# HGRN scans with the decays multiplied out ahead, the copy behind the query product, and 64 moving columns

## The reference

```python
def step(S, inp):
    qc, kc, vc, lc = inp
    bcum = jnp.cumsum(lc, axis=1)
    diff = bcum[:, :, None] - bcum[:, None, :]
    decay = jnp.where(lower, jnp.exp(jnp.where(lower, diff, 0.0)), 0.0)
    att = jnp.einsum('bthd,btshd->bths', qc, decay * kc[:, None])
    o = jnp.einsum('bths,bshv->bthv', att, vc) + jnp.einsum('bthd,bhdv->bthv', qc * jnp.exp(bcum), S)
    blast = bcum[:, -1]
    S_new = jnp.exp(blast)[..., None] * S + jnp.einsum('bshd,bshv->bhdv', kc * jnp.exp(blast[:, None] - bcum), vc)
    return S_new, o
```

## Time and profile before

| what | value |
|---|---|
| median of 3 runs | 2461.57 us |
| profiled execution, its own time | 2460.36 us |
| its span, first to last instruction | 2458.2 us |
| mean granted TensorE clock | 0.979 of full speed |
| TensorE matmul busy | 2296.2 us (93%) |
| VectorE busy | 1481.1 us (60%) |
| ScalarE busy | 832.3 us (34%) |
| POOL busy | 176.4 us (7%) |
| level matmuls (L789) | 1120 records, 291 ns of one |
| masked copies of the levels (L1819) | 140, 520 ns of one |
| decay products (L1823) | 120 on `tp` with 377 ns of one, 20 on `fg` |
| query products (L1825) | 120 on `tp` with 412 ns of one, 20 on `fg` |
| POOL's key products (L2149) | 120 on `tp` with 656 ns of one, 20 on `fg` with 854 |

### The profile page before, as it was taken

The page is one execution under the profiler, slowest core; times in us unless marked ns, Lnnn a source line. Parts: engine busy times, 40 slices in busy tenths (PEclk is TensorE's granted clock), DMA queues, the critical chain, the costliest instruction groups (busy, mean ns, idle before and its releaser), DMA issues.

```text
span 2458.2 us, 35437 instructions
## 1 busy us (share of the span) xinstructions
PE 2296.2 (93%) x14713; PEld 2019.9 (82%) x14713; DVE 1481.1 (60%) x2254; ACT 832.3 (34%) x1581; POOL 176.4 (7%) x217
## 2 busy tenths in 40 slices
PE   5989889988999889999999999999899999999998
PEld 3868868878888788779999999799555799999997
DVE  4457482257423777677555564789677575555655
ACT  4355372210122006444222222533455442222222
POOL 0000000023101330110000000200000100000002
PEclk9989999999999999999999999999999999999999
DMA  7411205510252002232222132131000022221321
GB/s 294 165 35 57 78 1 210 204 62 1 75 208 103 10 17 84 82 103 80 67 86 78 60 95 69 39 98 61 22 1 2 26 78 69 86 78 54 101 68 44
DMA packets 43854, 193.60 MB, mean 79 GB/s; under 512 B 5008, under 2 KB 5008, under 8 KB 36912
## 3 DMA queue, kind: packets, MB, share of 16 engines
q1 hardware_dynamic: 41472, 178.10, 21.5%
q0 software_dynamic: 2224, 13.24, 1.5%
HBM read 183.72 MB, written 7.60 MB: 78 GB/s over the span
## 4 chain that ended last, share of the span: by engine, by line
PE 81%; DVE 13%; ACT 3%; issue 2%; DMA 1%; SPq 0%; DVEq 0%; ACTq 0%
PE pg L843 30%; PE pg L882 17%; PE pg L638 16%; PE ps L789 3%; PE ps L1062 2%; PE pg L1042 2%; DVE att L1819 2%; PE ps L612 2%; DVE wk L1825 1%; PE ps L734 1%; PE pg L1017 1%; DMA ybuf<-in_wada 1%; DVE tp L1823 1%; PE ps L1017 1%; PE ps L753 1%
## 5 line engine op out<-in xcount | busy, mean ns | idle before, releaser
L843 PE MATMUL pg<-hh,xhi 128*128 128x320 f32 (+2 forms) x1008 | 314.4, 312 | 6.5 <-DVE hl L1635 6.5
L843 PE MATMUL pg<-hl,xhi 128*128 128x320 f32 (+2 forms) x1008 | 310.9, 308 | 0.0
L843 PE MATMUL pg<-hh,xlo 128*128 128x320 f32 (+2 forms) x1008 | 310.9, 308 | 0.0
L1521 DVE TENSOR_TENSOR wlo<-ring,whi 128x1024 fp32r<-128x1024 f32 x129 | 157.0, 1222 | 187.9 <-ACT whi L1105 187.7
L638 PE MATMUL pg<-hh,whi 128*128 128x320 f32 x976 | 238.8, 326 | 22.5 <-DVE hl L1553 9.5
L638 PE MATMUL pg<-hl,whi 128*128 128x320 f32 x976 | 225.5, 313 | 0.0
L638 PE MATMUL pg<-hh,wlo 128*128 128x320 f32 x976 | 225.1, 312 | 0.0
L638 PEld LDWEIGHTS pg<-hh,whi 128*128 128x128 f32 x976 | 165.2, 192 | 61.9 <-issue 51.4
L843 PE MATMUL pg<-hh,whi 128*128 128x320 f32 (+2 forms) x672 | 209.3, 311 | 3.3 <-DVE hl L1635 3.3
L843 PE MATMUL pg<-hl,whi 128*128 128x320 f32 (+2 forms) x672 | 207.2, 308 | 0.0
L843 PE MATMUL pg<-hh,wlo 128*128 128x320 f32 (+2 forms) x672 | 207.2, 308 | 0.0
(11 more groups left out here) (317 smaller groups left out, 4629.1 us busy)
## 6 DMA issues: line engine op xcount, KB each, us to landing
ring<-in_wstream SPq DMA_DIRECT2D x231, 512.0 KB, 3.7
adaring<-in_wada SPq DMA_DIRECT2D x21, 1024.0 KB, 5.0
ybuf<-in_wada SPq DMA_DIRECT2D x21, 1024.0 KB, 4.9
adabig<-in_wada SPq DMA_DIRECT2D x6, 1024.0 KB, 18.8
xk<-in_x SPq DMA_DIRECT2D x1, 2560.0 KB, 11.2
yssd_scratch<-ybuf POOLq DMA_DIRECT2D x2, 1280.0 KB, 5.8
xk<-yssd_scratch POOLq DMA_DIRECT2D x1, 2560.0 KB, 10.1
xk<-in_x_tok POOLq DMA_DIRECT2D x1, 2560.0 KB, 8.9
```

The source lines that it names most:

```text
L843: last = nc.tensor.matmul(out, w[:, k * P:(k + 1) * P], h[:, k, a:b], start=k == 0 and m == 0, stop=k == KT - 1 and m == 2)
L1521: V.tensor_tensor(lo, flat(ring[:, s % RING]), hi.bitcast(F32), ALU.subtract).then_inc(wlo_ready, 1)
```

## The change

Five things change in the scan.

The products of the gates of whole runs are no longer computed inside the levels. A new function `decays(p)` computes those of a whole pair of blocks: two products for level 1, one for each direction, and then one instruction for both directions at each further level. It runs before the first pair's `start`, and for every other pair at the end of the levels of the pair before. So that the old and the new products can stand side by side, they alternate between `tp` and a part of `sq` (`tps`).

The query product of a level stands ahead of the masked copy instead of behind it. It waits for the same `lv_ready`.

The matmul of a level takes as its moving side only the queries of the later runs, 64 columns a head instead of 128. Its output is packed: 64 columns a head.

The outputs of the levels alternate between two PSUM banks for each direction (`level_bank`), 0 and 2 of `ps` for direction 0, 1 and 3 for direction 1. Banks 2 and 3 also hold an output and a state sum, so TensorE waits at level 1 until the previous pair's are read. The diagonals move to bank 0 of `ps` for direction 0 and to the first bank of `pg` for direction 1.

A new semaphore, `lv_copied`, counts the masked copies. TensorE waits on it ahead of the diagonals and of the outputs; the copy of a level waits for that of the level before.

The diff:

```diff
@@ -308,6 +308,7 @@
             att = sb("att", [P, 2, HG_SET, P], F32, ph)
             hst = sb("hst", [P, 2, HG_SET, P], F32, ph)
             hfin = sb("hfin", [P, 2, HG_SET, P], F32, ph)
+        tps = [tp, flat(sq[:])[:, 0:2 * HG_SET * P].rearrange("p (d h t) -> p d h t", d=2, h=HG_SET)]
         qp = wk[:, 0:2, 0:HG_SET * P].rearrange("p d (h t) -> p d h t", h=HG_SET)
         ktok = wk[:, 2:4, 0:HG_SET * P].rearrange("p d (h t) -> p d h t", h=HG_SET)
         mask_in = ybuf[:, 0:2].rearrange("p f t -> p (f t)")[:, 0:2 * LEVELS * 64 + P]
@@ -476,6 +477,7 @@
         qp_ready = sem("qp_ready")
         dg_ready = sem("dg_ready")
         lv_ready = sem("lv_ready")
+        lv_copied = sem("lv_copied")
         kk_ready = sem("kk_ready")
         kt_ready = sem("kt_ready")
         kt_done = sem("kt_done")
@@ -542,10 +544,22 @@
 
             return ap.rearrange("p h (b t w) -> p h b t w", t=2, w=w)[:, :, :, t, :]
 
-        def tlevel(d, i):
+        def tlevels(np_, i):
 
             off = P - (P >> (i - 1))
-            return tp[:, d, :, off:off + (P >> i)]
+            return tps[np_ % 2][:, :, :, off:off + (P >> i)]
+
+        def tlevel(np_, d, i):
+
+            return tlevels(np_, i)[:, d]
+
+        def level_bank(d, i):
+
+            return ps[:, d + 2 * (i % 2), 0:HG_SET * 64]
+
+        def diagonal_bank(d):
+
+            return pg[:, 0, 0:512] if d else ps[:, 0, :]
 
         def mod_at(layer, part, ft, c):
             i = (layer * 6 + part) * KT + ft
@@ -768,8 +782,9 @@
                     for d in range(2):
                         if np_:
                             pe.wait_ge(qp_ready, qp_need(np_ - 1, 0, 0))
+                            pe.wait_ge(lv_copied, 2 * LEVELS * np_ - 1)
                         for h in range(HG_SET):
-                            last = nc.tensor.matmul(pg[:, 0, d * 512 + h * P:d * 512 + (h + 1) * P], kg[:, d, h, tok[d]],
+                            last = nc.tensor.matmul(diagonal_bank(d)[:, h * P:(h + 1) * P], kg[:, d, h, tok[d]],
                                                     qs[:, h, tok[d]], start=True, stop=True)
                         last.then_inc(dg_ready, 1)
 
@@ -780,14 +795,19 @@
                     if np_:
                         pe.wait_ge(o_done[1], np_)
                     for i in range(LEVELS):
+                        w = 1 << i
+                        if i == 1 and np_:
+                            pe.wait_ge(o_done[0], np_)
+                            pe.wait_ge(hs_done, 2 * (np_ - g) - 1 if p else 8)
                         for d in range(2):
                             n = (np_ * LEVELS + i) * 2 + d
                             pe.wait_ge(qp_ready, qp_need(np_, i, d))
                             if i:
                                 pe.wait_ge(kk_ready, n - 1)
                             for h in range(HG_SET):
-                                last = nc.tensor.matmul(ps[:, d, h * P:(h + 1) * P], kg[:, d, h, tok[d]],
-                                                        qp[:, d, h, :], start=True, stop=True)
+                                last = nc.tensor.matmul(level_bank(d, i)[:, h * 64:(h + 1) * 64]
+                                                        .rearrange("p (b w) -> p b w", w=w), kg[:, d, h, tok[d]],
+                                                        halves(qp[:, d], w, 1 - d)[:, h], start=True, stop=True)
                             last.then_inc(lv_ready, 1)
                     for d in range(2):
                         v = 2 * (np_ - g) + d
@@ -805,6 +825,7 @@
                     if p < len(HG_PAIRS) - 1:
                         diagonals(p + 1)
                     for d in range(2):
+                        pe.wait_ge(lv_copied, 2 * LEVELS * np_ + 2 * (LEVELS - 1) + d + 1)
                         if np_:
                             pe.wait_ge(o_done[d], np_)
                         if p == 1:
@@ -1792,6 +1813,19 @@
                 V.tensor_tensor(ybuf[:, 4 * g:4 * g + 4], ybuf[:, 4 * g:4 * g + 4], zs[:], ALU.mult).then_inc(yz_ready, 1)
 
             def hgrn(g):
+                def decays(p):
+
+                    np_ = g * len(HG_PAIRS) + p
+                    for d in range(2):
+                        tok = slice(HG_PAIRS[p][d] * P, (HG_PAIRS[p][d] + 1) * P)
+                        pairs = fg[:, d, :, tok].rearrange("p h (b t) -> p h b t", t=2)
+                        last = V.tensor_tensor(tlevel(np_, d, 1), pairs[:, :, :, 0], pairs[:, :, :, 1], ALU.mult)
+                    for i in range(1, LEVELS):
+                        link(last)
+                        pairs = tlevels(np_, i).rearrange("p d h (b t) -> p d h b t", t=2)
+                        last = V.tensor_tensor(tlevels(np_, i + 1), pairs[:, :, :, :, 0], pairs[:, :, :, :, 1], ALU.mult)
+                    link(last)
+
                 def start(p):
 
                     np_ = g * len(HG_PAIRS) + p
@@ -1802,9 +1836,10 @@
                         V.tensor_tensor(qp[:, d], qs[:, :, tok], fg[:, d, :, tok], ALU.mult).then_inc(qp_ready, 1)
                         dve.wait_ge(dg_ready, 2 * np_ + d + 1)
                         V.copy_predicated(att[:, d], m8[:, 2 * LEVELS * 64:].unsqueeze(1).broadcast_to([P, HG_SET, P]),
-                                          pg[:, 0, d * 512:(d + 1) * 512]
-                                          .rearrange("p (h t) -> p h t", h=HG_SET)).then_inc(qp_ready, 1)
-
+                                          diagonal_bank(d).rearrange("p (h t) -> p h t", h=HG_SET)
+                                          ).then_inc(qp_ready, 1)
+
+                decays(0)
                 start(0)
                 for p, pair in enumerate(HG_PAIRS):
                     np_ = g * len(HG_PAIRS) + p
@@ -1816,14 +1851,18 @@
                             dve.wait_ge(lv_ready, n + 1)
                             mo = (d * LEVELS + i) * 64
                             mask = m8[:, mo:mo + 64].rearrange("p (b w) -> p b w", w=w).unsqueeze(1)
+                            decay = fg[:, d, :, tok[d]] if i == 0 else tlevel(np_, d, i)
+                            decay = decay.rearrange("p h (b t) -> p h b t", t=2)[:, :, :, d]
+                            q = halves(qp[:, d], w, 1 - d)
+                            V.tensor_tensor(q, q, decay.unsqueeze(3).broadcast_to([P, HG_SET, 64 // w, w]),
+                                            ALU.mult).then_inc(qp_ready, 1)
+                            if i:
+                                dve.wait_ge(lv_copied, n - 1)
                             V.copy_predicated(halves(att[:, d], w, 1 - d), mask.broadcast_to([P, HG_SET, 64 // w, w]),
-                                              halves(ps[:, d].rearrange("p (h t) -> p h t", h=HG_SET), w, 1 - d))
-                            tot = fg[:, d, :, tok[d]] if i == 0 else tlevel(d, i)
-                            pairs = tot.rearrange("p h (b t) -> p h b t", t=2)
-                            V.tensor_tensor(tlevel(d, i + 1), pairs[:, :, :, 0], pairs[:, :, :, 1], ALU.mult)
-                            q = halves(qp[:, d], w, 1 - d)
-                            V.tensor_tensor(q, q, pairs[:, :, :, d].unsqueeze(3)
-                                            .broadcast_to([P, HG_SET, 64 // w, w]), ALU.mult).then_inc(qp_ready, 1)
+                                              level_bank(d, i).rearrange("p (h b w) -> p h b w", h=HG_SET, w=w)
+                                              ).then_inc(lv_copied, 1)
+                    if p < len(HG_PAIRS) - 1:
+                        decays(p + 1)
                     for d in range(2):
                         v = 2 * np_ + d
                         if d == 1 and p < len(HG_PAIRS) - 1:
@@ -1849,7 +1888,7 @@
                             dve.wait_ge(hst_in, 16 * (g + 1))
                             for h in range(HG_SET):
                                 last = V.scalar_tensor_tensor(out=hst[:, d, h], in0=hst[:, d, h],
-                                                              scalar=tlevel(d, LEVELS)[:, h], in1=src[:, h],
+                                                              scalar=tlevel(np_, d, LEVELS)[:, h], in1=src[:, h],
                                                               op0=ALU.mult, op1=ALU.add)
                             last.then_inc(hs_done, 1)
 
@@ -2143,7 +2182,7 @@
                             n = (np_ * LEVELS + i) * 2 + d
                             tok = slice(pair[d] * P, (pair[d] + 1) * P)
                             pool.wait_ge(lv_ready, n + 1)
-                            tot = fg[:, d, :, tok] if i == 0 else tlevel(d, i)
+                            tot = fg[:, d, :, tok] if i == 0 else tlevel(np_, d, i)
                             tot = tot.rearrange("p h (b t) -> p h b t", t=2)[:, :, :, 1 - d]
                             k = halves(kg[:, d, :, tok], w, d)
                             G.tensor_tensor(k, k, tot.unsqueeze(3).broadcast_to([P, HG_SET, 64 // w, w]),
```

## The result

The changed kernel takes 2521.73 us, the median of 4 runs (2519.38 to 2526.02), beside 2462.12 us before (4 runs). The ratio is 1.0244, 95% interval 1.0226 to 1.0262: 59.6 us slower, where 2436 us and a gain of 26 was forecast. The outcome is rival C, a lower TensorE clock.

The account below looks back on a forecast made before the run. In the scans TensorE and VectorE were both taken as nearly full, alternating in each level's chain, with POOL beside them. Savings of 20 and 5.6 us summed to 25.6, giving a median of 2436 us, range 2418 to 2456.

Parts of the forecast that it names:

- rival C: TensorE's clock in the scans falls to 1.2 GHz; 40 levels at that clock give 30 us slower, 2492; chance 0.09.
- Item 2: Level matmuls with 64 moving columns: the weight load sets the step, so only 0.05 us saved per direction, bounds 0 to 0.45.
- Item 1: Levels 1 to 6: query product before copy, decays out, POOL held 0.25 us; 12.94 instead of 14.04, 1.10 us a pair.
- Item 3: Level 0 of the third pair: query product first saves 1.23 and 1.44 us by direction; with levels 2.54 a pair.
- Item 4: Second pair of each half: query product ready before POOL's DMAs, less TensorE idle; 2.8 us a pair, bounds 1.9 to 3.6.
- Item 5: Decays ahead, 2.5 us a block, hide in VectorE's idle time between pairs and before the first pair: cost 0.
- Item 6: New waits, copies before diagonals and outputs and level 1 into banks 2 and 3: cost 0.
- A: No collisions in the levels: POOL is not set back, each of 60 levels gains 0.25 more, 15 us, 2421; chance 0.15.
- B: Levels keep 2.34 us because POOL and VectorE collide more than once; only level 0 gains, 13, 2449; chance 0.16.
- D: Decays don't hide at the start of a pair: 25 us back, 2461, no change; chance 0.05.
- forecast: The main case for the whole kernel: 25.6 us saved, 2436 us, own spread 2430 to 2443; chance 0.55.

Follow-up runs that it names:

- mixed run: Changed kernel with 128 moving columns at levels 0, 2, 4 and 6 and 64 at levels 1, 3 and 5: 2448.41 us, ratio 0.9943.
- run 16: Not a run's label: in "the mixed run 16 records take 1.97 us" the 16 counts matmul records; the run meant is the mixed run.
- 128-column kernel: Changed kernel with the level matmuls back at 128 moving columns a head, outputs unpacked, two banks and new order kept: 2442.45 us, ratio 0.9923.
- decays in PSUM: With 64 columns: the kernel with early first-pair decays and the query product's decays copied to PSUM, given the changed kernel's matmul: 2500.91 us, ratio 1.0159.
- PSUM run: Kernel with 128 columns and each half's first decays early, plus the decays the query product reads copied into a free PSUM bank: 2431.09 us, ratio 0.9865.
- key first: Kernel with 128 columns, masked copy ahead of the query product again, so POOL's key product starts first: 2446.49 us, ratio 0.9936.

## Why the prediction was wrong, point by point

**Item 2 is the step that failed.** It valued 64 columns at -0.05 us a direction, "the weight load of 128 columns sets the step, not the moving side, and it stays". That holds at 2.4 GHz: in the changed kernel's level 1 and in the narrow levels of the mixed run 16 records take 1.97 us, and eight of them 1.09 (585.89) instead of 1.14 with 128 columns, 0.05 less as forecast. But it priced the instruction and not the clock, and its bounds, 0 to 0.45 a direction, had no loss in them. In the levels that follow the step is 0.21 us instead of 0.11. The record says where: level matmuls 146.2 us with 128 columns, 216.2 with 64, 70 us more, less 8.7 of idle time that they now fill. A level at the low clock has 3.4 us of records instead of 2.0, so 70 / 1.4 makes about 50 of the 70 levels; 841 of the 1120 level records start at the low clock. The transposes and diagonals behind them, which start at the low clock, are slower too (the transposes take 17.2 us, L822, and 10.0 with 128 columns, L821). Narrow columns cost 79 us, for a gain of 0.05 us where the clock held.

**Rival C had the right result and too small a chance.** It took 40 levels at 1.4 us and came to 2492; it was some 50, at 1.24 over levels 2 to 6 ((17.17 - 10.97) / 5), and the rest of the pair besides. I named half the columns and the gaps together. Undoing the columns alone brings the clock back in both orders, so without the narrow side there is no loss; but the gaps are not ruled out as its partner. The third pair from level 1 on, changed kernel and then 128-column kernel:

```profile
585.89 1.97 PE L808 MATMUL ps<-wk,kg 128*128 128x64 f32 x16 [0.57 <-DVE wk L1857]
...
588.25 17.17 PE L808 MATMUL ps<-wk,kg 128*128 128x64 f32 x80 [0.39 <-POOL kg L2188]
```
```profile
568.08 2.02 PE L808 MATMUL ps<-wk,kg 128*128 128x128 f32 x16 [0.57 <-DVE wk L1856]
570.44 2.02 PE L808 MATMUL ps<-wk,kg 128*128 128x128 f32 x16 [0.34 <-POOL kg L2187]
```

The same waits stand in both, and only the narrow kernel falls, within half a microsecond of 588.25. That the slow stretch behind it has no gap is a result of the low clock. In the changed kernel every fall comes between level 0 and level 3, where TensorE still waits for VectorE or POOL, and with the decays in PSUM 64 columns once ran 11.7 us at 1.00 almost without a gap. What the runs show is that with these waits among them the narrow records lose the clock in pair after pair and the wide ones nearly never (31 of their 1120 records start at the low clock, all in the two first pairs); whether narrow ones without any wait would lose it, only that one pair speaks to, and it speaks against.

My argument against C, that the clock stayed at 1.00 through 1.60 us of waiting, was about gaps between records of 128 columns. The nearest rows to a narrow matmul have 128 columns or more too: I used no stretch with 64, so nothing there could speak against the half of C that the change brought in. The Trainium skill (TensorE: Matmul & The Clock Gate, HAM oscillation) describes the loss of clock through idle gaps of the engine; here waits of 0.57 and 0.39 us came before the fall, and waits as long cost nothing with 128 columns.

**Item 1** was right in its mechanism and wrong in size. VectorE is first and POOL is held: 0.87 against 0.63, 0.24 instead of 0.25, and the PSUM run removes it. In the third pair of the 128-column kernel levels 2 to 5 start 2.26, 2.24, 2.23 and 2.21 us apart, not 12.94 / 6 = 2.16. The term that is off is POOL's hand-over to TensorE, taken as 0.05 and measured as 0.14 (in the chain of the changed kernel from 588.11 to 588.25, and as much in the 128-column kernel); over six levels and ten pairs 0.09 is 5 us. The masked copy, taken to cost nothing, does stand in the chain at the first levels of the second pairs (four times 0.64 us from 541.55 on, ahead of query products). The Trainium skill's rule (SBUF — State Buffer, Who interferes with whom) that the pair is exclusive while VectorE reads two SBUF inputs holds in all three forms tried: query first, key first, one operand in PSUM. In the changed kernel item 1 gains nothing in the slow levels, because there a level waits for TensorE.

**Item 3**: with 128 columns level 0 of the third pair takes 2.52 us instead of 3.55, 1.03 saved of the 1.23 for direction 0, and its seven levels 15.85 (581.41 - 565.56) instead of 17.70, 1.85 saved of 2.54. The chain goes on through direction 0 (569.29, POOL's key product behind the first eight records of level 1), not through direction 1 with its 1.44 as the sum had it. **Item 4**: in the 128-column kernel the second pair's levels keep their clock, and TensorE's idle time in the stretch of the DMAs is 1.0 of 2.50 us, where it was all of it. From its first to its last level record the pair takes 16.69 us instead of 19.75, 3.1 saved of 2.8: right.

```profile
542.50:545.00 2.50, 1.49 (x12) 1.47 (x13) 2.50 (x3) 0.00 (x0) 1.92 (x3) 1.00 0.56 210
```

**Item 5** was right between pairs and wrong before the first: "0" was 1.15 us in the first half, since the block stands behind the wait for the values and not in the idle time before it; in the second half it was a level 0 at the low clock, 3.44 us instead of 2.44. **Item 6** was right: in the chains that I read no output or diagonal waits for the new semaphores. Without item 2 the change gains 20 us instead of 25.6; item 1's hand-over (5) and the first pairs (2, by medians whose runs overlap) cover that difference, with nothing left for level 0, so these parts are rough.

**Rivals A, B and D** didn't come, as the 128-column kernel shows: POOL is set back in nearly every level (a median of 0.87), levels 1 to 6 gain, and the decays hide between the pairs. The chances have a slip: forecast, A and B add up to 0.86 with nothing taken off for a weaker B.

## What to carry to other kernels

Where the weight load sets the step of a matmul, a narrower moving side has next to nothing to give, and it can lose the clock: with 64 fp32 columns and waits of half a microsecond among them TensorE fell to 1.2 GHz in all ten pairs and stayed there while its records ran without a gap. So keep dead columns where the weight load hides them, and after any edit that thins matmuls read the granted clock of the stretch before anything else. Where VectorE and GpSimd work side by side and both are on the path, moving one of VectorE's operands to PSUM can be worth the copy that it takes: here it gave 9 us.

## What the runs showed of the hardware

- The same level matmuls lost the clock or kept it by their moving columns: at 64 most of their records start at 0.50 (841 of 1120), at 80 a third (386), at 96 and 128 few (32 and 31; 46 in the kernel before); 2521.7, 2474.4, 2442.6 and 2442.5 us. It is not the columns alone: with 80 the first two pairs of each half fell and the last three didn't, and with the decays in PSUM one pair of ten kept 1.00 with 64.
- A busy TensorE in the profile can be a slow one: 10.01 us of records in 10.01 us are 81 records at 1.00, and 17.17 in 17.17 are 81 records at 0.50.
- GpSimd to TensorE takes 0.14 us (588.11 to 588.25 in the changed kernel), VectorE to TensorE 0.04 (580.98 to 581.03 with the copy first).
- A VectorE product of 256 elements with one operand in PSUM took 0.42 us (median of 120), against 0.43 with both in SBUF, and never more than 0.46 beside GpSimd, against up to 0.86.
- The masked copy of 256 elements takes 0.70 to 0.75 us at levels 0 and 1 and 0.43 from level 2 on, packed source or not (medians of 140: 435 ns packed in the changed kernel, 435 unpacked in the 128-column kernel).
